# Two products of 256 columns in place of one of 512, in the gate and up products of a feed-forward stage

## The reference

```
x = x + 0.5 * swiglu(rms_norm(x, ffn1_norm), gate, up, down)
h = rms_norm(x, mix_norm) @ w_in       # three token mixers, merge, w_out, residual
x = x + 0.5 * swiglu(rms_norm(x, ffn2_norm), gate, up, down)

def swiglu(x, w_gate, w_up, w_down):
    return (jax.nn.silu(x @ w_gate) * (x @ w_up)) @ w_down
```

## Time and profile before

| what | value |
|---|---|
| median of 3 runs | 1189.84 us |
| span of the profiled execution, first to last instruction | 1187.9 us |
| PE busy | 1175.4 us (99%), 6442 matmuls |
| weight loads (PEld) | 967.1 us (81%), 6442 |
| DVE busy | 976.4 us (82%) |
| ACT busy | 616.1 us (52%) |
| POOL busy | 74.9 us (6%) |
| granted clock of TensorE, mean | 0.998 |

### The profile page before, as it was taken

How to read it: one execution, slowest core, us unless ns; L and a number is a source line. 1 busy time by engine, 2 the same in 40 slices (tenths; PEclk the granted TensorE clock), 3 DMA queues, 4 the chain that set the end, 5 groups by cost and what they waited for, 6 DMA issues and landing times.

```text
span 1187.9 us, 18888 instructions
## 1 busy us (share of the span) xinstructions
PE 1175.4 (99%) x6442; PEld 967.1 (81%) x6442; DVE 976.4 (82%) x2103; ACT 616.1 (52%) x1045; POOL 74.9 (6%) x151
## 2 busy tenths in 40 slices
PE   8999999999999999999999999999999999999997
PEld 7888888887778888888888888888877888888886
DVE  7988886678878698888788898875889696988886
ACT  6544446556654454444464444465566535444443
POOL 5300000421000000000000000024100000000000
PEclk9999999999999999999999999999999999999999
DMA  9655554553445465455565555535543554655553
GB/s 377 231 188 177 200 190 164 186 178 115 144 178 177 177 212 196 176 209 181 208 219 206 201 187 212 182 142 186 173 148 112 196 194 153 231 191 201 209 179 142
DMA packets 37143, 223.53 MB, mean 188 GB/s; under 512 B 6752, under 2 KB 9440, under 8 KB 11232
## 3 DMA queue, kind: packets, MB, share of 16 engines
q1 hardware_dynamic: 35360, 216.36, 51.4%
q10 hardware_dynamic: 1696, 6.43, 1.6%
q0 software_dynamic: 32, 0.00, 0.0%
HBM read 218.58 MB, written 1.05 MB: 185 GB/s over the span
## 4 chain that ended last, share of the span: by engine, by line
PE 86%; DVE 9%; ACT 3%; issue 2%; DMA 0%; DVEq 0%; ACTq 0%
PE G L1430 21%; PE G L1431 21%; PE G L1432 21%; DVE wlo L960 3%; PE TO L1432 3%; PE TO L1431 3%; PE TO L1430 3%; PE SC L1432 3%; PE SC L1431 3%; PE SC L1430 3%; ACT probs L765 2%; DVE sm L1188 1%; DVE probs L1215 1%; PE TO L1446 1%; PE TO L1707 1%
## 5 line engine op out<-in xcount | busy, mean ns | idle before, releaser
L960 DVE TENSOR_TENSOR wlo<-raw,whi 128x1024 fp32r<-128x1024 f32 x395 | 468.2, 1226 | 114.6 <-ACT whi L579 112.4
L579 ACT ACTIVATE whi<-raw 128x1024 fp32r<-128x1024 f32 x395 | 396.2, 1053 | 266.8 <-PE G L1432 149.2
L1430 PE MATMUL G<-whi,xhi 128*128 128x512 f32 x1184 | 464.4, 392 | 1.2 <-DVE wlo L1023 0.7
L1432 PE MATMUL G<-whi,xlo 128*128 128x512 f32 x1184 | 458.2, 387 | 0.0
L1431 PE MATMUL G<-wlo,xhi 128*128 128x512 f32 x1184 | 458.1, 387 | 0.0
L1430 PEld LDWEIGHTS G<-whi,xhi 128*128 128x128 f32 x1184 | 222.9, 188 | 54.4 <-issue 5.4
L1432 PEld LDWEIGHTS G<-whi,xlo 128*128 128x128 f32 x1184 | 222.8, 188 | 45.6
L1431 PEld LDWEIGHTS G<-wlo,xhi 128*128 128x128 f32 x1184 | 223.0, 188 | 43.3
L1054 DVE STREAM_TRANSPOSE shared_q<-shared_q 32x128 f32<-32x128 f32 x640 | 193.7, 303 | 8.3
L651 ACT ACTIVATE shared_q<-G,stat 128x256 f32<-128x256 f32 x88 | 41.8, 476 | 78.1 <-PE G L1432 75.5
L1430 PE MATMUL TO<-whi,ybhi 128*128 128x512 f32 x176 | 69.0, 392 | 0.0
(11 more groups left out here) (204 smaller groups left out, 968.5 us busy)
## 6 DMA issues: line engine op xcount, KB each, us to landing
raw<-stream SPq DMA_DIRECT2D x200, 1024.0 KB, 4.8
gates<-w_in ACTq DMA_DIRECT2D x2, 2048.0 KB, 8.6
z<-z SPq DMA_DIRECT2D x32, 64.0 KB, 4.2
x<-x_in SPq DMA_DIRECT2D x4, 256.0 KB, 5.8
raw<-stream SPq DMA_DIRECT2D x2, 512.0 KB, 5.7
small<-small_in ACTq DMA_DIRECT2D x2, 414.5 KB, 3.1
const<-const_in SPq DMA_DIRECT2D x1, 690.0 KB, 11.9
z<-zkv SPq DMA_DIRECT2D x32, 16.0 KB, 2.0
```

Source lines behind the costliest of these rows:

```text
L579: act.activation(whi[s][:, c], raw[s][:, c], ACT.Copy).then_inc(hi_done, 1)
L960: dve.tensor_tensor(wlo[s][:, c], raw[s][:, c], whi[s][:, c].bitcast(F32), ALU.subtract).then_inc(lo_done, 1)
L1430: pe.matmul(o, ahi, bhi, start=first, stop=False)
L1432: return pe.matmul(o, alo, bhi, start=False, stop=last)
```

## The change

In chunks 1 to 10 of every feed-forward stage each product of 512 columns is issued as two of 256, one for the left half of the bank (gate) and one for the right half (up), with the same stationary tile and the same order of parts. Only the first of all products of a bank has the start flag; the second half goes without it. Chunk 0, the down products and the mixer call `mm3` as before.

```diff
+NARROW = 256
...
+            def mm3_narrow(o, ahi, alo, bhi, blo, first, last):
+
+                for a, b in ((ahi, bhi), (ahi, blo), (alo, bhi)):
+                    for c in range(0, 512, NARROW):
+                        ins = pe.matmul(
+                            o[:, c : c + NARROW], a, b[:, c : c + NARROW],
+                            start=first and a is ahi and b is bhi and c == 0, stop=last and a is alo,
+                            skip_group_check=True)
+                return ins
+
-            def gemm_half(o, tok, hi, lo, k0, s, n, first, last, unit=None, before=None):
+            def gemm_half(o, tok, hi, lo, k0, s, n, first, last, unit=None, before=None, product=mm3):
...
-                    ins = mm3(
+                    ins = product(
...
-                            unit=None if tok or very_first else unit, before=lifted if peeled else None)
+                            unit=None if tok or very_first else unit, before=lifted if peeled else None,
+                            product=mm3 if peeled else mm3_narrow)
```

## The result

The changed kernel takes 1215.63 us, the median of 4 runs (1215.29 to 1215.9), beside 1189.94 for the kernel before on the same chip: a ratio of 1.0218, 95% interval 1.0206 to 1.023, 25.7 us more. The forecast was 1197.7; rival A had 1215.7.

A forecast was written before the change was run, and what follows sets the result against it. PE was taken to bound the kernel through the step between matmuls, 226.8 ns per wide product. 1920 pairs times 4.1 ns gave 7.9 us, added to the 1189.84 median: 1197.7 us, range 1186 to 1217.

The forecast's parts named there:

- rival A: Feed-forward pairs: all 13.5 ns of excess come once per product, 25.9 us more, 1215.7 us; chance 0.17.
- 1920 pairs: Chunks 1 to 10 of four feed-forward stages: 1920 wide G products become 3840 of 256 columns.
- two loads for each: Each pair loads its stationary tile twice, 1920 more loads in all, 8362 in place of 6442.
- room on every other engine: Feed-forward loop: a later PE gives VectorE, ACT and transfers more room; VectorE has 2.3 us per turn now.
- a floor under a narrow step: Feed-forward narrow products: the weight load keeps a step from falling below 108 to 111 ns.
- what streaming 256 columns costs: Narrow step: 0.435 ns per column plus 4.1 once, 115.5 ns; 4.1 more per pair, 7.9 us in all.
- The once-only bound of 0: Lower bound for a pair: 0.443 ns per column, nothing once per product, so a pair costs 0 more.
- The line to 125.6: Upper bound from 220-column and wide steps: 125.6 ns per narrow step, 24.4 more per pair.
- Rival C: Feed-forward pairs: excess purely per column, a pair costs what the wide product did, 0 to 2 us; chance 0.16.
- rival D: Feed-forward pairs: excess belongs to long streams, narrow products step at the load's floor, -7.7 to -19.6 us; chance 0.12.
- I take 0: First wide down products behind narrow ones, 40 places: no extra cost taken, at most 1.2 us kept for the range.
- Strict P: Strict form of the experiments' theory P, for chunks 1 to 10: 13.3 ns once per product wherever operands lie.

The follow-up runs named there:

- e2: Changed kernel with pairs cut at column 256, 320, 384, 448 by stage: 1282.63 us (one run); pairs 240, 258.0, 285.4, 311.6 ns.
- e5: Changed kernel with only some products narrow: one or two of three per group, second token tile alone, none, by stage: 1200.96 us, ratio 1.0093.
- e8: Kernel before, moving columns starting 8 or 16 words in, or tile shifted 16 or 64 words, by stage; tile-shifted steps 231.4 and 226.7 ns.
- e10: Changed kernel with the stationary tile shifted 8, 16, 32, 64 words by stage: narrow steps 118.1, 117.8, 120.0, 119.9 ns.
- e6: Changed kernel with one product of 248, 264, 272, 496 columns by stage, other columns left out: steps 115.7, 119.9, 125.3, 220.0 ns.
- e7: Changed kernel with one 256-column product starting at column 0, 4, 16, 136 by stage, other half left out: steps 120.0, 118.7, 117.8, 116.7 ns.
- e9: Kernel before, wide products, stationary tile shifted 4, 32, 48, 24 words by stage: steps 226.7, 232.4, 231.1, 234.0 ns.
- e1: Changed kernel with each group of six reordered, left halves first, tile changed at every step but one: 1215.31 us, ratio 1.0218.

## Why the prediction was wrong

Right: 1920 pairs; two loads for each, against the words of the change; no new wait, no loading of code, room on every other engine; a floor under a narrow step, put at 108 to 111 ns, where the short halves of e2 take 111 to 113. The sign was right, and A stood among the rivals with its price. That this price comes within 0.1 us of the median is in part luck: it has 13.5 ns for 13.3, and nothing for the places where narrow and wide products meet.

Wrong is the step "what streaming 256 columns costs". It took 389 and 262 ns as two points of one line and got 0.435 ns per column and 4.1 once. Measured in series, the slope is the clock's: (226.7 - 120.0) / 256 = 0.4167, and what comes once is 13.3, not 4.1. The 262 ns are right for what they are, the first short product behind a wide one, and a first product of 256 columns took 277 where the line gave 278. But e5 shows that such a product leaves its cost to those behind it: the wide products behind a lone pair step 233 in place of 227. So a pair was put at 4.1 ns, 7.9 us in all, where it costs 13.3, 25.6 in all. The prediction said that no row shows a 256-column product of this kind in series; it then gave the row that was exact to the nanosecond more weight than the long straight series of wide steps, which could be read only one way if the columns cost what the clock says.

The other terms, in order. The once-only bound of 0 rested on the same four places, so it was no second witness. The line to 125.6 was too high: the 220-column step of 111.4 is the load's floor. Rival C put the excess on the columns and rival D on long streams, and neither fits 13.3 at both widths; float32's small excess, which D built on, doesn't carry over to a stream at the full rate. e8 to e10 move a step by up to 7 ns by the place of the tile alone, which is read when it is loaded, so the load and the stream beside it are not independent. The rule of the Trainium skill that the prediction named ("TensorE: Matmul & The Clock Gate", section "Step-by-step: what each phase is for"), that loading the next weights takes no read bandwidth from the running matmul, is not borne out by this. "I take 0" for the first wide products should have been the 1.2 us.

Strict P falls too. The 13.3 ns belong to this kernel's layout, where every moving slice and every tile starts on a multiple of 128 words, and to widths like 256, 496 and 512: in the same layout e6 has 9.9 to 12.4 at other widths. Elsewhere the excess of an fp32r product with a whole tile over its streaming was 10.0 (e7, column 136: 116.7 - 106.7) to 20.7 ns (e9, 24 words: 234.0 - 213.3). For this change the size stands: it was measured in that layout at both widths, and e1, e2 and e7's first stage give it again.

Open: which resource tile and columns compete for. The runs show that a stream at half the rate loses 2.5 ns with the same load beside it, that the places of tile and columns count, and that shifting the tile by 64 words changes nothing. No run has a stream without a load. They don't show why half a tile costs a wide product more, why some widths cost less than 13.3, or why lone pairs cost more than pairs in series.

## What to carry to other kernels

A price for a series is read from a series: the first instruction of a kind behind another kind can be cheap because those behind it pay. A steady step minus its streaming time is taken as a cost per instruction until a second width in series says otherwise, and halving the products doubles it. Words like "on the same stationary tile" are checked against the count of loads.

## Not expected of the hardware

A step between full-rate products depends on where tile and columns lie: 226.7 to 234.0 ns for the same wide product, 116.7 to 120.0 for the same narrow one. Some cases repeat to the nanosecond (220.0, 120.0), others in short cycles (117, 123). A tile of 64 columns made pairs of 256 cheap (113.4) and products of 512 dear (230.0).
